# Stick-breaking layer of a two-layer trunk: the adaLN sum of layer 1 in 128x512 slices on VectorE, and the head sum kept in PSUM

## What is computed

```python
cond = silu(c)
for i in range(2):
    ada = cond @ w_ada[i] + b_ada[i]
    shift, scale, gate = split(ada, 3)
    h = rms_norm(x, g_pre[i]) * (1.0 + scale) + shift
    u = h @ w_in[i]
    mix_in, z = u[..., :3072], u[..., 3072:]
    y = stick_breaking_attention(mix_in) if i == 0 else diff_attention(mix_in, ...)
    y = (y * silu(z)) @ w_out[i]
    x = x + gate * rms_norm(y, g_post[i])
```

```python
log_beta = log_sigmoid(logits)
log_keep = where(strict, log_beta - logits, 0.0)
between = cumsum(log_keep, reverse=True) - log_keep
weights = where(strict, exp(log_beta + between), 0.0)
out = weights @ v
```

## Time and profile before

| | us |
|---|---|
| median of 3 runs (lowest to highest) | 1553.54 (1553.09 to 1553.61) |
| the profiled execution | 1552.89 |
| its span | 1551.0 |
| PE busy in it | 1382.5 (89%) |
| DVE busy | 1057.0 (68%) |
| ACT busy | 879.3 (57%) |
| POOL busy | 554.8 (36%) |

### The profile page before, as it was taken

One profiled execution on the slowest core, in us unless ns is written; L12 is line 12 of the kernel. 1 busy time (PEld: TensorE's weight loads), 2 busy tenths in 40 slices (PEclk: granted clock), 3 DMA queues, 4 the chain that ended last, 5 costly groups with the idle time before them and its releaser, 6 DMA issues. The chain is left out here.

```text
span 1551.0 us, 23600 instructions
## 1 busy us (share of the span) xinstructions
PE 1382.5 (89%) x7154; PEld 1138.9 (73%) x7154; DVE 1057.0 (68%) x1824; ACT 879.3 (57%) x1712; POOL 554.8 (36%) x325
## 2 busy tenths in 40 slices
PE   4688999999999999986997899999999999995898
PEld 2567777777777777775875678887877888784776
DVE  4868888797979797978457656556565656557415
ACT  4346555565656565555445467667676757667322
POOL 1024555555646564636222322121122212122204
PEclk9899999999999999996998899999999999996999
DMA  9012111102021111122034001100100010002014
GB/s 342 28 41 64 46 54 52 56 27 80 28 68 41 54 54 54 54 73 90 1 112 146 28 28 32 37 27 27 41 27 27 27 39 28 27 14 109 0 58 174
DMA packets 112649, 89.82 MB, mean 58 GB/s; under 512 B 2553, under 2 KB 101090, under 8 KB 112610
## 3 DMA queue, kind: packets, MB, share of 16 engines
q1 hardware_dynamic: 112320, 89.15, 18.3%
q10 hardware_dynamic: 290, 0.18, 0.1%
HBM read 80.92 MB, written 8.40 MB: 58 GB/s over the span
## 5 line engine op out<-in xcount | busy, mean ns | idle before, releaser
L674 PE MATMUL bank<-h_hi,w_hi 128*128 128x512 f32 x976 | 396.0, 406 | 9.1 <-POOL h_lo L583 4.5
L674 PE MATMUL bank<-h_lo,w_hi 128*128 128x512 f32 x976 | 393.2, 403 | 0.0
L674 PE MATMUL bank<-h_hi,w_lo 128*128 128x512 f32 x976 | 390.7, 400 | 0.0
L644 POOL TENSOR_TENSOR w_lo<-w_raw,w_hi 128x1024 fp32r<-128x1024 f32 x59 | 159.4, 2701 | 374.6 <-ACT w_hi L638 374.5
L1288 POOL TENSOR_TENSOR a<-a,stick 128x128 f32<-128x128 f32 (+7 forms) x128 | 189.6, 1486 | 251.0 <-DVE stick L1153 251.0
L1153 DVE TENSOR_TENSOR_SCAN stick<-b 128x128 f32<-128x128 f32 (+7 forms) x128 | 204.1, 1594 | 41.4 <-ACT b L1057 41.4
L674 PEld LDWEIGHTS bank<-h_hi,w_hi 128*128 128x128 f32 x976 | 185.9, 190 | 41.6 <-issue 10.0
L674 PEld LDWEIGHTS bank<-h_hi,w_lo 128*128 128x128 f32 x976 | 185.5, 190 | 33.1
L674 PEld LDWEIGHTS bank<-h_lo,w_hi 128*128 128x128 f32 x976 | 185.5, 190 | 30.4
L1056 ACT ACTIVATE a<-bank 128x512 f32<-128x512 f32 (+2 forms) x192 | 94.7, 493 | 90.5 <-PE bank L960 52.6
L1069 ACT ACTIVATE wt_hi<-bank 128x512 fp32r<-128x512 f32 (+2 forms) x192 | 87.8, 494 | 74.8 <-PE bank L976 73.0
(11 more groups left out here) (215 smaller groups left out, 3036.8 us busy)
## 6 DMA issues: line engine op xcount, KB each, us to landing
w_raw<-in_w_in_dram SPq DMA_DIRECT2D x63, 512.0 KB, 4.0
ada_piece<-in_w_ada_dram SPq DMA_DIRECT2D x32, 512.0 KB, 3.8
p_ada<-in_w_ada_dram SPq DMA_DIRECT2D x8, 1024.0 KB, 13.2
wo_raw<-in_w_out_dram SPq DMA_DIRECT2D x8, 1024.0 KB, 9.9
p_x<-in_x_dram SPq DMA_DIRECT2D x8, 512.0 KB, 7.7
o_x<-in_x_dram SPq DMA_DIRECT2D x8, 512.0 KB, 4.1
x_between<-o_res SPq DMA_DIRECT2D x8, 512.0 KB, 2.9
o_x<-x_between SPq DMA_DIRECT2D x8, 512.0 KB, 4.1
```

The costliest lines, as they stand in the source:

```text
L644: self.nc.gpsimd.tensor_tensor(self.m["w_lo"][s][:, :, :], self.m["w_raw"][s][:, :, :], self.m["w_hi"][s][:, :, :].bitcast(F32), ALU.subtr ...
L674: mm = nc.tensor.matmul(self.bank[half][:, :], w[:, k, :], h[:, k, half * HALF:(half + 1) * HALF], start=(i == 0), stop=(i == GROUP - 1))
```

## The change

The work on w_ada is cut along other lines. A pair now deals with 512 columns as eight slices k of 128 rows by 512 columns (`ada_slice`, 256 KB each). At each odd step 1 to 15 DVE multiplies slice k by its column of cond and adds it to `ada_acc` in one instruction; the slice k = 0 starts the sum with a `tensor_scalar`. POOL's multiplication and its semaphore are gone. PE's four one-column matmuls of a pair stand together ahead of group 7 and DVE adds four columns in one instruction. Layer 1's 3072 columns take six pairs, which are now the loop (`LOOPED` = 6), and the gate of layer 0 pairs 6 and 7. Pair 6 is written out behind the loop, as pair 7 was.

The head sum stays in PSUM: DVE adds `O` and `o_part` back into `O`, and the gating product reads `O`. So PE's next group waits for the product (`y_done`), and ACT's next copy only for the sum (`summed`). A tile is renamed (`ada_sum` to `vectors`), which the prologue uses.

The core of the diff:

```diff
@@ block.sync
-            def ada(p, i):
-                layer, at = (1, (3 * p + i) * P) if i < 3 else (0, 2 * D + p * P)
-                sp.wait_ge(ada_summed, done(ADA * p + i - 1))
-                sp.dma_start(m["ada_piece"][:, :, :], w_ada[layer, :, bass.ds(at, P)]
-                             .rearrange("(k p) f -> p k f", p=P)).then_inc(ada_in, 16)
-
-            with sp.Fori(0, PAIRS - 1) as p:
+            def ada(p, *ks):
+                layer, at = (0, 2 * D + (p - LOOPED) * HALF) if isinstance(p, int) else (1, p * HALF)
+                for k in ks:
+                    sp.wait_ge(ada_summed, done(KT * p + k - 1))
+                    sp.dma_start(m["ada_slice"][:, :], w_ada[layer, k * P:(k + 1) * P, bass.ds(at, HALF)]
+                                 ).then_inc(ada_in, 16)
+
+            def pair(p):
                 proj.load(sp, p + 1, 0)
-                ada(p, 0)
+                ada(p, 0, 1)
                 proj.load(sp, p + 1, 1)
-                ada(p, 1)
-                ada(p, 2)
+                ada(p, 2, 3, 4)
                 proj.load(sp, p + 1, 2)
-                ada(p, 3)
+                ada(p, 5, 6, 7)
                 proj.load(sp, p + 1, 3)
-            for i in range(2):
-                ada(PAIRS - 1, i)
+
+            with sp.Fori(0, LOOPED) as p:
+                pair(p)
+            for p in range(LOOPED, PAIRS - 1):
+                pair(p)
+            ada(PAIRS - 1, 0, 1, 2, 3, 4)
 
             sp.wait_ge(proj.group_done, done(8 * PAIRS - 1))
             outp.load_weights(sp, w_out)
-            for i in range(2, ADA):
-                ada(PAIRS - 1, i)
+            ada(PAIRS - 1, 5, 6, 7)
@@ block.tensor, values
-                pe.wait_ge(summed, done(GROUPS * p + g - 1))
-                if g % 2:
...
+                pe.wait_ge(y_done, done(GROUPS * p + g - 1))
+                if g == GROUPS - 1:
+                    pe.wait_ge(ada_summed, done(KT * p + KT - 1))
+                    for j in range(HALF // P):
+                        mm = nc.tensor.matmul(O[:, GW + j:GW + j + 1], m["ada_acc"][:, j * P:(j + 1) * P],
+                                              m["ones"][:, 0:1], start=True, stop=True)
+                    mm.then_inc(ada_done, 1)
@@ block.scalar, other_part
-                act.wait_ge(y_done, done(GROUPS * p + g - 1))
+                act.wait_ge(summed, done(GROUPS * p + g - 1))
@@ block.vector, add_parts
-                nc.vector.tensor_tensor(m["o_part"][own, :], O[own, 0:GW], m["o_part"][own, :],
-                                        ALU.add).then_inc(summed, 1)
+                nc.vector.tensor_tensor(O[own, 0:GW], O[own, 0:GW], m["o_part"][own, :], ALU.add).then_inc(summed, 1)
                 dve.wait_ge(summed, done(GROUPS * p + g))
...
-                nc.vector.tensor_tensor(y, m["o_part"][own, :], y, ALU.mult).then_inc(y_done, 1)
+                nc.vector.tensor_tensor(y, O[own, 0:GW], y, ALU.mult).then_inc(y_done, 1)
@@ block.vector, sum_ada
+            def sum_ada(p, k):
+                acc, cond = m["ada_acc"][:, :], m["cond"][:, k:k + 1]
+                dve.wait_ge(ada_in, 16 * (KT * p + k) + 16)
+                if k == 0:
+                    dve.wait_ge(ada_done, done(p - 1))
+                    ins = nc.vector.tensor_scalar(acc, m["ada_slice"][:, :], cond, None, ALU.mult)
+                else:
+                    dve.wait_ge(ada_summed, done(KT * p + k - 1))
+                    ins = nc.vector.scalar_tensor_tensor(out=acc, in0=m["ada_slice"][:, :], scalar=cond, in1=acc,
+                                                         op0=ALU.mult, op1=ALU.add)
+                ins.then_inc(ada_summed, 1)
...
-                    if s % 4 == 3 and s // 4 < ADA:
-                        sum_ada(p, s // 4)
+                    if s in ADA_AT:
+                        sum_ada(p, ADA_AT[s])
@@ block.gpsimd
-            def scale_ada(p, i):
...
-                    if s % 4 == 1 and s // 4 < ADA:
-                        scale_ada(p, s // 4)
```

More of the change, by code:

```diff
@@ L116, in trunk @@
     m["uv"] = sb("uv", [P, S], F32, 120)
-    m["ada_piece"] = sb("ada_piece", [P, KT, P], F32, 124)
+    m["ada_slice"] = sb("ada_slice", [P, HALF], F32, 124)
+    m["ada_acc"] = sb("ada_acc", [P, HALF], F32, 126)
     m["z_sig"] = sb("z_sig", [P, S], F32, 124)
@@ L154, in trunk @@
     m["add_col"] = [small(f"add_col{l}", [P, KT], F32, 4 * KT) for l in range(DEPTH)]
-    m["ada_sum"] = small("ada_sum", [P, P], F32, 4 * P)
+    m["vectors"] = small("vectors", [P, P], F32, 4 * P)
     m["lam"] = small("lam", [P, 8], F32, 32)
@@ L210, in __init__ @@
         self.scale1 = sb("p_scale1", [P, KT], F32, 127.75)
-        self.vec = m["ada_sum"]
+        self.vec = m["vectors"]
         self.vec_t, self.row = m["pm"][2], m["pm"][5]
@@ L892, in stick_breaking @@
     zsig, one_set, summed = sem("zsig"), sem("one_set"), sem("summed")
-    ada_in, ada_done, ada_kept = sem("ada_loaded"), sem("ada_done"), sem("ada_kept")
-    ada_scaled, ada_summed = sem("ada_scaled"), sem("ada_summed")
+    ada_in, ada_summed, ada_done, ada_kept = sem("ada_loaded"), sem("ada_summed"), sem("ada_done"), sem("ada_kept")
     chain, gate_turned, gate_kept = sem("chain"), sem("gate_turned"), sem("gate_kept")
     gate_rows_sb = m["o_part"]
-    ADA = 4
+    ADA_AT = {2 * k + 1: k for k in range(KT)}
+    LOOPED = 3 * D // HALF
     pack = Packing(nc, m, "s")
@@ L1033, in _ @@
             pro.tensor(pe)
-            with pe.Fori(0, PAIRS - 1) as p:
+            with pe.Fori(0, LOOPED) as p:
+                pair(p, True)
+            for p in range(LOOPED, PAIRS - 1):
                 pair(p, True)
@@ L1132, in _ @@
                     proj.split_hi(act, 0, 3)
-            with act.Fori(0, PAIRS - 1) as p:
+            with act.Fori(0, LOOPED) as p:
+                pair(p, True)
+            for p in range(LOOPED, PAIRS - 1):
                 pair(p, True)
@@ L1171, in add_parts @@
                 dve.wait_ge(part_done, done(GROUPS * p + g))
[L1172 to L1177, removed]
-                nc.vector.tensor_tensor(m["o_part"][own, :], O[own, 0:GW], m["o_part"][own, :],
-                                        ALU.add).then_inc(summed, 1)
+                if g == GROUPS - 1:
+                    n = HALF // P
+                    at = 2 * KT + n * (p - LOOPED) if isinstance(p, int) else 3 * KT + n * p
+                    dve.wait_ge(ada_done, done(p))
+                    cols = m["ada_cols"][:, :, :].rearrange("p l f -> p (l f)")[:, bass.ds(at, n)]
+                    nc.vector.tensor_tensor(cols, O[:, GW:GW + n], cols, ALU.add).then_inc(ada_kept, 1)
+                nc.vector.tensor_tensor(O[own, 0:GW], O[own, 0:GW], m["o_part"][own, :], ALU.add).then_inc(summed, 1)
                 dve.wait_ge(summed, done(GROUPS * p + g))
                 y = m["y"][own, :, :].rearrange("r k t -> r (k t)")[:, bass.ds(p * S + gg * GW, GW)]
-                nc.vector.tensor_tensor(y, m["o_part"][own, :], y, ALU.mult).then_inc(y_done, 1)
+                nc.vector.tensor_tensor(y, O[own, 0:GW], y, ALU.mult).then_inc(y_done, 1)
             def z_gate(p, half):
@@ L1209, in finish_ada @@
                 tt = nc.vector.tensor_tensor
-                dve.wait_ge(ada_kept, done(ADA * PAIRS - 1))
+                dve.wait_ge(ada_kept, done(PAIRS - 1))
                 link(nc.vector.scalar_tensor_tensor(out=m["mul_col"][1][:, :], in0=ada[:, 4 * KT:5 * KT], scalar=1.0,
@@ L1269, in _ @@
                 keep_u(0, 2, half)
-            with dve.Fori(0, PAIRS - 1) as p:
+            with dve.Fori(0, LOOPED) as p:
+                pair(p, True)
+            for p in range(LOOPED, PAIRS - 1):
                 pair(p, True)
@@ L1277, in _ @@
         def _(pool):
-            for q in (proj.lo_done, weighted, ada_scaled):
+            for q in (proj.lo_done, weighted):
                 pool.sem_inc(q, CREDIT)
@@ L1310, in _ @@
             proj.split_lo(pool, 0, 3)
-            with pool.Fori(0, PAIRS - 1) as p:
+            with pool.Fori(0, LOOPED) as p:
+                pair(p, True)
+            for p in range(LOOPED, PAIRS - 1):
                 pair(p, True)
```

9 lines of the change are left out of this document (removed).

## The result

| | before | after |
|---|---|---|
| time, median of four runs | 1553.57 us (1553.09 to 1554.47) | 1585.15 us (1582.07 to 1588.43) |
| ratio | 1 | 1.0205, 95% interval 1.0193 to 1.0217 |
| span of the profiled execution | 1551.0 us | 1586.6 us |
| a pair of the loop (pair 2) | 81.3 us | 85.2 us |
| last pair, start to end | 113.6 us | 121.1 us |

The change costs 31.6 us, clear of the noise; 1548.8 was forecast. In the profiled execution, the longest of its four (1588.43 us), the loop has lost 26.6 us, the last pair 7.5, and all behind it 1.5. The loop is measured between PE's first scores of pairs 0 and 7, the last pair from there to the end of VectorE's last record in it (786.68 and 820.87 us).

What follows compares the result with a forecast made beforehand. PE was taken to bound the loop, busy 75.27 of 81.30 us a pair, its seven waits the gap. 1552.89 - 10.0 (loop) + 5.3 (last pair) = 1548.2 us profiled, forecast as 1548.8, range 1534 to 1562.

Steps and rivals of the forecast that it cites:

- Gating from PSUM, about 420 ns: VectorE's gating product L1182 falls from 951 to about 420 ns when reading PSUM, 4.2 us of VectorE per pair.
- the fixed cycles of PSUM: Gating products: 120 fixed cycles from PSUM against 58 from SBUF, an estimated 0.5 us more per pair.
- Pair loop, wait by wait, -1.43 us a pair: PE's waits in a loop pair: 1.56 added at step 5, 0.62, 0.99 and 1.38 gone; seven pairs -10.0 us.
- the wait that "stays" at 0.69: PE's wait at 289.16 in the loop pair, 0.69 us: before anything that moved, so unchanged.
- The waits of 296.99, 308.38 and 334.28: PE's loop-pair waits of 0.62, 0.99 and 1.38 us: gone, through POOL's scaling removed or the faster gating product.
- that of 326.99: PE's loop-pair wait of 0.71 us: little changes, as the sum of step 13 meets another w_lo.
- these seven: PE's seven waits in a loop pair, 5.96 us together, the whole gap: the loop's effect is what happens to them.
- Who shares with POOL: POOL and a VectorE instruction with two SBUF inputs run one at a time; one PSUM input takes VectorE out.
- What does not share: VectorE's old reductions, four per pair at 1960 ns, did not have to share with POOL; the new sums do.
- Last pair, +5.3: w_out's loads start 10.7 us late, ScalarE's queue stands 8.7, and scan 8 and the end move by +5.3 us.
- C: Rival, slower: loop sums and POOL wait on each other until nothing is saved, w_out late; 1558.8 us, chance 0.22.
- B: Rival, full relief: no collision at step 5 and three loop waits go, -20.9 + 5.3; 1537.9 us, chance 0.2.

Runs made afterwards that it cites:

- The first run: Kernel before with only the head sum kept in PSUM and read there by the gating product: 1547.17 us, ratio 0.9963.
- run 5: Kernel after, with POOL's split of step 15 held behind the first key copy and the last pair's w_out loads ahead of slice 2: 1549.77 us.
- run 4: Kernel after, with POOL's split of step 15 waiting until the first key copy is done: 1550.64 us, ratio 0.9989.
- the ninth kernel: Kernel after, sums at steps 0, 1, 2, 3, 7, 9, 11, 12, and POOL's low halves of kinds 1 and 2 one step later: 1550.26 us.
- runs 2: Kernel after with the head sum in SBUF again, leaving the slices alone: 1586.98 us, ratio 1.0217.
- run 3: Kernel after, with w_out's loads issued ahead of slice 2 in the last pair: 1581.64 us, ratio 1.0185.
- the seventh run: Kernel before plus an unused VectorE reduction at step 15 of the seven loop pairs: 1580.99 us, ratio 1.0174.
- the sixth run: Kernel after with the eight sums at steps 0, 1, 2, 3, 7, 9, 11, 12 and w_out's loads behind slice 3: 1532.72 us, ratio 0.9862.
- the eleventh: Kernel before with only POOL's low halves of kinds 1 and 2 one step later: 1557.01 us, ratio 1.0021.
- tenth kernels: Kernel before plus the useless VectorE reduction at step 15, with POOL's split there waiting for the first key copy: 1554.98 us, ratio 1.0013.
- the twelfth kernel: Kernel after with sums moved off steps 5, 13, 15, POOL's kinds 1 and 2 one step later, wt_lo ahead of the first key low part: 1527.28 us.

## Why the prediction was wrong

The forecast was 1548.8 us with a range of 1534 to 1562; 1585.15 lies outside. Its own steps, one by one:

- *Gating from PSUM, about 420 ns*: right (422 and 434 ns). The first run puts this part alone at -6.3 us. The prediction set beside it the fixed cycles of PSUM from the Trainium skill, VectorE: DVE Perf Modes, its section on the TRN2 errata, an estimated 3.6 us over seven pairs. The trace does not agree: the gating product from PSUM takes 422 ns, and the same product from SBUF took 417 ns in the kernel before where POOL was idle.
- *Pair loop, wait by wait, -1.43 us a pair*: the sum was right (-1.37), its parts only in part. At step 5 VectorE did the sum at 295.46 while POOL's product ran until 296.91; that product took 2.74 us and PE waited for it one product earlier than forecast: the wait that "stays" at 0.69 became 1.83 (297.04), and the wait after it is 1.46 instead of 2.55. That the total fits is luck in part. The waits of 296.99, 308.38 and 334.28 went, that of 326.99 stayed (0.72).
- *The step that failed* is the frame of that sum: "what the change does for the loop is what it does to these seven". VectorE's sum of step 15 was in the count of VectorE's work (+0.74 us) and was never followed to what stood behind it. PE already stood some 0.2 us for the `wt_lo` there, in no list, and the two instructions that decide the rest were 0.05 us apart. The term left out is +2.81 us of stop and some 3 us of low clock a pair; a price for the clock stood nowhere in the sum. With the order held the loop gains 10.2 us in the trace of run 5, and 2.0 in that of run 4, where the clock stayed low for longer: the term left out is the loop's miss, whole or nearly so. For the clock: from the column matmuls to the first 128x512 row takes 5.18 us in the kernel after (350.57 to 355.75) and 2.83 in pair 2 of the ninth kernel, which has the same instructions at the full clock (339.69 to 342.52), so 2.35, and the next three 128x512 rows take 0.21 to 0.34 more each. Over the whole pair PE is busy for 77.76 us instead of 75.27, 2.49 more.
- *Who shares with POOL*: "a VectorE instruction with two SBUF inputs" was too narrow. The copy has one input in SBUF and one output there, and takes 2.74 to 2.80 us behind POOL instead of 0.69 in five kernels (after, and runs 2, 3, 7 and 9). The trace of the kernel before had shown it, in the prologue:
```profile
97.52 3.43 POOL L644 TENSOR_TENSOR w_lo<-w_raw,w_hi 128x1024 fp32r<-128x1024 f32 x1 [35.55 <-ACT w_hi L638]
...
98.77 2.73 DVE L736 CAST k_lo<-k_lo 64x1024 fp32r<-64x1024 f32 x1
```
- *What does not share*: VectorE's reductions keep their time beside POOL, as the forecast had it: L1195 takes 1.91 us at 332.50 in the kernel before, while POOL's products run from 330.39 to 336.10, and 1.91 to 2.01 in all 32 places.
- *Last pair, +5.3*: the rows fit the mechanism. w_out's first issue came 8.7 us later in the pair where 10.7 was worked out, ScalarE's stop was 9.96 us where 8.7 was; the start of the output products moved by 5.2. That the end would move as much was wrong: POOL's `wo_lo` is late too, and the pair lost 7.5. How much of it is w_out's is open: 3.2 of the 7.5 go with run 4, which leaves w_out late, and run 3 paid for early w_out with a late slice.
- *The rivals*: C named the sign, and the wrong places: sums against POOL at steps 5 and 13. By the Trainium skill, Perfetto Trace Analysis, Optimizing Scalar/DVE Operations, moving work between GpSimd and VectorE might not help. As a warning it agrees with the result, but it does not decide: the same moved work gives 1585 us and, at other steps, 1533 and 1527. B's 1537.9 is near the sixth run's 1532.7, for another reason: there the sums do not stand at steps 5, 13 and 15.

What is shown and what is not: the order of copy and `w_lo` is shown as the cause of the loop's loss, by the kernel after with the order held (-34.5 us), by the kernel before with the order turned (+27.4), by the same delay with the order held (+1.5), and by pair 6 of the ninth run. Why the clock falls behind some waits and not behind others of the same length stays open.

## What to carry to other kernels

Beside the list of waits, make a list of near misses: for each instruction that the slowest engine needs, how long it was ready ahead of time, and which two instructions of engines that slow each other start within a few tenths of each other. Take the distance between the starts of matmuls for this, not the idle time in the list: 0.46 us where 0.23 is the rule was PE waiting, though the list showed nothing. An edit that shifts one engine by some tenths of a microsecond is to be followed through that list, not only through the waits that exist. Where such a pair stands ahead of something critical, fix its order: a semaphore wait or the exchange of two instructions made it safe here, and was worth more than the work saved.

## What the hardware showed that was not expected

- 5.6 us of work on VectorE cost 27.4 us (the seventh run), because an order turned; it had moved the copy by 0.22 us.
- The clock behind a short stop is not settled by its length. Behind 2.81 and 2.37 us the rows were at half clock in pair 2 of the kernels after and before-plus-delay. Behind 2.38 us in pair 2 of the ninth kernel they were not; behind 2.36 in its pair 4 they were, from 2.2 us after the wait on. Behind 0.71 they were in the eleventh and tenth kernels, and not in the kernel before (0.69). So removing waits can leave less than their sum: the twelfth kernel has rows of 0.63 us behind its wait of 1.12.
- A 256 KB slice, which takes 2.7 us from issue to landing in the median of the kernel after, kept VectorE waiting for 6.56 us when 4 MB of another tensor stood ahead of it in the same queue (third run).
